# Hybrid decoder layer: three pieces of the closing RMS norm move from VectorE to GpSimd and ScalarE, and VectorE's last operations change order

## The chip, the cores and the metric

The kernel is written in Bass for one Trainium2 chip and runs on one core. The metric is the device time of one execution in microseconds, the median over runs.

## The reference

One decoder layer over 512 tokens of 1024 features in float32: block-sparse attention and a spatial-gating mixer side by side, an output projection, a squared-ReLU MLP, and last a gated per-layer embedding. Only the last three lines bear on the change:

```python
gate = jax.nn.sigmoid(jnp.einsum('bsd,de->bse', h, w_ple_gate[i]) + b_ple_gate[i])
ple = jnp.einsum('bsp,pd->bsd', p[i], w_ple[i]) * gate
h = h + rms_norm(ple, ple_post_g[i])
```

`rms_norm(x, g)` is `x * rsqrt(mean(x*x) + 1e-6) * g`, the mean over a token's 1024 features.

## The kernel before, in words

Each engine has one hand-written queue of instructions and runs it in order; semaphores tie the queues together (`wait_ge` in front of an instruction, `then_inc` behind it). Products of full float32 accuracy are made of three passes on TensorE over high and low parts. ScalarE makes the high parts, VectorE the low ones. The MLP and the gate product use a seven-product scheme over halves of tokens and features, so VectorE and ScalarE also make sums of blocks all through.

The end of the kernel is what the change touches. The gate's result, 4 groups of 128 tokens (t = 0 to 3) by 1024 columns, is finished in nine tiles, the table `GATE_TILES` (number: token group, first column): 0: t0, 0; 1: t1, 0; 2: t2, 512; 3: t2, 0; 4: t3, 512; 5: t0, 512; 6: t3, 0; 7: t1, 512; 8: t1, 768. Tiles 7 and 8 have 256 columns, the rest 512. Tile numbers follow the order in which TensorE completes them. Per tile there are six steps:

1. `sigmoid(i)` on ScalarE (L2242), out of PSUM.
2. `gate_ple(i)` on VectorE (L1463), the "gate product": sigmoid times the embedding product (`ple_late_a` for t0 and t1, `ple_late_b` for t2 and t3). Its result lies in `acc` (SBUF) for tiles 0 and 1 and in PSUM for the others.
3. `square_ple(i)` on ScalarE (L1620): sum of squares, an ACTIVATE with an accumulator read behind it.
4. On GpSimd (POOL) `partial_sum` (L2512), and once per token group `ple_rstd(t)` (L2518, L2520): 1/rms of the group's tokens, in the order t = 2, 0, 3, 1. It needs the last square of the group: 3, 5, 6, 8.
5. The "weight product": times the norm weights `ple_gain`. `gain_ple(i)` on VectorE (L1474) for tiles 2 to 8, `gain_by_pool(i)` on POOL (L2531) for tiles 0 and 1, written over `ple_late_a`.
6. `add_ple(i)` on VectorE (L1486), the "last step": h = weight product * 1/rms + h, in one scalar_tensor_tensor.

Ahead of this end VectorE runs low parts (L1409, L1432, L1376), `gate_c22` (L1440, a subtraction that completes tiles 2 and 4, the second once TensorE's product (4, 1) is done) and `gate_fold` (L1448, L1452, L1454). SyncE (SP) stores one tile per DMA (L2689), each behind its last step, in the order of `add_ple`, all on one queue. The order of all these is a list of calls per engine:

Of the kernel before, what the change touches and what calls it, by code (L numbers as in the profile page):

```python
# [35 lines left out]
ALU = mybir.AluOpType  # L36
ACT = mybir.ActivationFunctionType
# [34 lines left out]
LAST = STEPS - 1  # L72
# [16 lines left out]
GATE_COPIES = ((COPY_C11, 0), (COPY_C11, 1), (COPY_E, 0), (COPY_CHAIN, 0), (COPY_CHAIN, 1), (COPY_E, 1))  # L89
# [22 lines left out]
def gate_copy_at(which, j):  # L112

    return 3 * LAST + GATE_COPIES.index((which, j)) + 1


def gate_c22_at(j):
# [173 lines left out]
TOKENS_DONE = (2, 0, 3, 1)  # L291
# [1 line left out]


LAST_GATED = len(GATE_TILES) - 1
GAINED_BY_POOL = (0, 1)


def width_of(i):
# [16 lines left out]
def hymba_layer(nc, x, xT, pT, weights, columns, rope, ws, rows, out):  # L316
# [6 lines left out]
    with ExitStack() as ctx:  # L323
# [31 lines left out]
        h = place("h", [P, TT, D])  # L355
# [65 lines left out]
        acc = place("acc", [P, TT, D], at=at_area)  # L421
# [40 lines left out]
        def ple_of(t):  # L462
            return ple_late[t // 2][:, t % 2, :]
# [28 lines left out]
        def sem(name):  # L492
            return ctx.enter_context(nc.semaphore(name))
# [60 lines left out]
        first_load = 16  # L554
        h2_raw, gate_seeded, gate_folded = sem("h2_raw"), sem("gate_seeded"), sem("gate_folded")
        h_spilled = sem("h_spilled")
        gained_by_pool = sem("gained_by_pool")
# [165 lines left out]
        def gate_result(i):  # L723

            t, c0, width = GATE_TILES[i]
            if i == LAST_GATED:
                return psum[:, GATE_LAST_PART, 0:width]
            if t < 2:
                bank = GATE_E if c0 else GATE_P1
            else:  # L730
                bank = GATE_C22 if c0 else GATE_CHAIN
            return psum[:, bank + t % 2, 0:width]

        def gated_of(i):

            t, c0, width = GATE_TILES[i]
            return acc[:, t, 0:W] if i < 2 else gate_result(i)

        def gained_of(i):

            t, c0, width = GATE_TILES[i]
            return ple_of(t)[:, c0:c0 + width] if i in GAINED_BY_POOL else gate_result(i)

        def down_result(t):

# [9 lines left out]
        def _(dve):  # L755
# [701 lines left out]
            def gate_ple(i):  # L1457
                t, c0, width = GATE_TILES[i]
                cut = slice(c0, c0 + width)
                dve.wait_ge(sig_done, i + 1)  # L1460
                if i in (0, 2):
                    dve.wait_ge(ple_loaded[t // 2], 16)
                nc.vector.tensor_tensor(gated_of(i), gated_of(i), ple_of(t)[:, cut], ALU.mult).then_inc(pl_gated, 1)  # L1463

            GAINED = (2, 3, 4, 5, 6, 7, 8)

            def gain_ple(i):

                if i == GAINED[0]:
                    dve.wait_ge(post_loaded, 48)  # L1470
                t, c0, width = GATE_TILES[i]
                cut = slice(c0, c0 + width)
                dve.wait_ge(pl_squared, i + 1)
                nc.vector.tensor_tensor(gained_of(i), gated_of(i), ple_gain[:, cut], ALU.mult  # L1474
                                        ).then_inc(pl_gained, 1)

            def add_ple(i):

                t, c0, width = GATE_TILES[i]
                cut = slice(c0, c0 + width)  # L1480
                dve.wait_ge(pl_rstd, TOKENS_DONE.index(t) + 1)
                if i in GAINED_BY_POOL:
                    dve.wait_ge(gained_by_pool, GAINED_BY_POOL.index(i) + 1)
# [60 lines left out]
            h2_sum_split_lo(OF_S4, 1)  # L1544
            gate_ple(2)
            gate_fold(1)
            gain_ple(2)
            gate_c22(1)
            gate_ple(3)
            gate_ple(4)  # L1550
            gain_ple(3)
            gain_ple(4)
            gate_ple(5)
            add_ple(2)
            add_ple(3)
            gain_ple(5)
            gate_ple(6)
            add_ple(0)
            gate_ple(7)
            add_ple(5)  # L1560
            gain_ple(6)
            gate_ple(8)
            gain_ple(7)
            add_ple(4)
            gain_ple(8)
            add_ple(6)
            add_ple(1)
            add_ple(7)
            add_ple(8)


# [3 lines left out]
        def _(act):  # L1575
# [659 lines left out]
            def sigmoid(i):  # L2235
                t, c0, width = GATE_TILES[i]
                j = t % 2
                if t >= 2 and c0:
                    act.wait_ge(c_summed, gate_c22_at(j))
                else:  # L2240
                    act.wait_ge(up_filled, gate_at(6 if c0 else 1 if t < 2 else 5, j) + (i == LAST_GATED))
                nc.scalar.activation(gated_of(i), gate_result(i), ACT.Sigmoid).then_inc(sig_done, 1)  # L2242
# [59 lines left out]
            gate_copy(COPY_E, 1)  # L2302
            square_ple(0)
            square_ple(1)
            square_ple(2)
            sigmoid(3)
            sigmoid(4)
            square_ple(3)
            square_ple(4)
            sigmoid(5)  # L2310
            square_ple(5)
            sigmoid(6)
            sigmoid(7)
            square_ple(6)
            sigmoid(8)
            square_ple(7)
            square_ple(8)

# [4 lines left out]
        def _(pool):  # L2323
# [200 lines left out]
            def gain_by_pool(i):  # L2524
                t, c0, width = GATE_TILES[i]
                cut = slice(c0, c0 + width)
                if i == 0:
                    pool.wait_ge(post_loaded, 48)
                    pool.wait_ge(sum_lo_done, gate_sum_split_at(OF_S4, 1))
                pool.wait_ge(pl_gated, i + 1)  # L2530
                nc.gpsimd.tensor_tensor(gained_of(i), gated_of(i), ple_gain[:, cut], ALU.mult  # L2531
                                        ).then_inc(gained_by_pool, 1)

            partial_sum(0)
            partial_sum(1)
            gain_by_pool(0)
            gain_by_pool(1)
            partial_sum(2)
            ple_rstd(2)
            partial_sum(4)  # L2540
            ple_rstd(0)
            ple_rstd(3)
            partial_sum(7)
            ple_rstd(1)

# [4 lines left out]
        def _(sp):  # L2550
# [134 lines left out]
            order = (2, 3, 0, 5, 4, 6, 1, 7, 8)  # L2685
            for n, i in enumerate(order):
                t, c0, width = GATE_TILES[i]
                sp.wait_ge(out_ready, n + 1)
# [596 lines left out]
```

## Time and profile before

| | |
|---|---|
| median of 3 runs | 579.03 us (578.3 to 579.38) |
| profiled execution, its own time | 578.58 us |
| its span | 576.7 us |
| TensorE busy | 568.4 us, 99% |
| VectorE busy | 500.8 us, 87% |
| ScalarE busy | 374.9 us, 65% |
| GpSimd busy | 96.2 us, 17% |
| mean granted TensorE clock | 0.996 of full speed |

A start time and a duration on a timeline are microseconds; consecutive instructions of one engine overlap a little, so the step from start to start is shorter than the duration. The span runs from the first to the last recorded event; the execution's own time is about 1.8 us longer. "x2" merges two neighbours with one name and gives their time from first start to last end. SPq and POOLq are the queues' own records of issuing a DMA.

### The profile page before, as it was taken

The page shows a single profiled execution, that of the slowest core. Times are in us where ns is not written, and L with a number is a line of the kernel's source. Part 1 is how long each engine was busy: PE and PEld are TensorE (multiplying, and loading weights), DVE is VectorE, ACT ScalarE, POOL GpSimd, SP SyncE. Part 2 cuts the span into 40 slices and gives each one's busy share as a digit, 9 for nine tenths or more (in the row PEclk, how much of TensorE's full clock was granted, in tenths as well). Part 3 has the DMA queues.
Part 4 walks back from the last instruction along what each step waited for, and adds up shares of the span by engine and source line. Part 5 has one row for each costly group of instructions (what it writes and reads, how often), then busy time and mean ns, then how long its engine had stood idle before and what let it go on. Part 6 is the DMA issues. An engine that isn't in the chain of part 4 may idle for free.

```text
span 576.7 us, 8934 instructions
## 1 busy us (share of the span) xinstructions
PE 568.4 (99%) x3364; PEld 496.3 (86%) x3364; DVE 500.8 (87%) x645; ACT 374.9 (65%) x595; POOL 96.2 (17%) x159
## 2 busy tenths in 40 slices
PE   9999999999999999999999999999999999999995
PEld 7888888888888888899999989999998999988884
DVE  5899986688865998999999989999999899798898
ACT  6896674876555747667565565665665656686784
POOL 0321437000102501001000010011010100014122
PEclk9999999999999999999999999999999999999998
DMA  8982008223103497367476384592774853897823
GB/s 268 346 324 90 0 2 321 82 73 108 41 1 110 147 349 233 74 195 207 74 249 154 73 266 100 147 255 44 236 167 77 268 124 78 324 265 144 227 112 148
DMA packets 28603, 93.73 MB, mean 163 GB/s; under 512 B 3216, under 2 KB 4624, under 8 KB 28304
## 3 DMA queue, kind: packets, MB, share of 16 engines
q1 hardware_dynamic: 20736, 67.64, 33.0%
q0 software_dynamic: 5328, 19.14, 18.8%
q10 hardware_dynamic: 2496, 6.37, 3.1%
q8 instruction: 27, 0.44, 0.3%
q14 instruction: 16, 0.13, 0.1%
HBM read 86.85 MB, written 6.29 MB: 161 GB/s over the span
## 4 chain that ended last, share of the span: by engine, by line
PE 93%; DVE 3%; ACT 1%; issue 1%; DMA 1%; DVEq 0%; SPq 0%; ACTq 0%
PE psum L2703 29%; PE psum L2707 29%; PE psum L2708 29%; PE psum L2758 2%; PE psum L2941 2%; PE psum L2921 2%; DVE h L1486 1%; DMA first_raw_a<-weights_dram 1%; PE psum L2772 1%; DVE w_lo L1376 1%; DVE psum L1474 1%; DVE psum L1463 0%; ACT junk_late L1620 0%; PE psum L2795 0%; DVE actT_lo L1432 0%
## 5 line engine op out<-in xcount | busy, mean ns | idle before, releaser
L2703 PE MATMUL psum<-t_hi,a_hi 128*128 128x512 f32 x216 | 84.7, 392 | 0.0
L2707 PE MATMUL psum<-t_lo,a_hi 128*128 128x512 f32 x216 | 84.6, 392 | 0.0
L2708 PE MATMUL psum<-t_hi,a_lo 128*128 128x512 f32 x216 | 84.0, 389 | 0.0
L2703 PE MATMUL psum<-w_hi,actT_hi 128*128 128x512 f32 (+1 forms) x178 | 69.7, 392 | 0.0
L2708 PE MATMUL psum<-w_hi,actT_lo 128*128 128x512 f32 (+1 forms) x178 | 68.5, 385 | 0.0
L2707 PE MATMUL psum<-w_lo,actT_hi 128*128 128x512 f32 (+1 forms) x178 | 68.4, 384 | 0.0
L2708 PE MATMUL psum<-sum_hi,up_lo 128*128 128x256 f32 x224 | 63.4, 283 | 0.0
L2707 PE MATMUL psum<-sum_lo,up_hi 128*128 128x256 f32 x224 | 63.4, 283 | 0.0
L2703 PE MATMUL psum<-sum_hi,up_hi 128*128 128x256 f32 x224 | 63.2, 282 | 0.0
L2708 PE MATMUL psum<-actT_hi,up_lo 128*128 128x256 f32 (+1 forms) x200 | 60.0, 300 | 0.0
L2707 PE MATMUL psum<-actT_lo,up_hi 128*128 128x256 f32 (+1 forms) x200 | 60.0, 300 | 0.0
L2703 PE MATMUL psum<-actT_hi,up_hi 128*128 128x256 f32 (+1 forms) x200 | 59.9, 299 | 0.0
L2454 POOL DMA_DIRECT2D raw_x<-weights_dram x21 | 18.6, 883 | 238.6 <-DVE t_lo L1235 238.6
L1294 DVE TENSOR_TENSOR acc<-acc,psum 128x512 f32<-128x512 f32 x76 | 49.1, 681 | 1.8 <-PE psum L2708 1.8
L2708 PEld LDWEIGHTS psum<-t_hi,a_lo 128*128 128x128 f32 x216 | 40.6, 188 | 8.8
L1090 DVE TENSOR_TENSOR up_lo<-raw,up_hi 128x1024 fp32r<-128x1024 f32 x37 | 45.2, 1220 | 2.6 <-ACT up_hi L1881 2.0
L2703 PEld LDWEIGHTS psum<-t_hi,a_hi 128*128 128x128 f32 x216 | 40.8, 189 | 7.1
L2707 PEld LDWEIGHTS psum<-t_lo,a_hi 128*128 128x128 f32 x216 | 40.8, 189 | 6.6
L2707 PEld LDWEIGHTS psum<-sum_lo,up_hi 128*128 128x128 f32 x224 | 42.9, 191 | 1.1
L2703 PEld LDWEIGHTS psum<-sum_hi,up_hi 128*128 128x128 f32 x224 | 42.9, 191 | 1.1
L2708 PEld LDWEIGHTS psum<-sum_hi,up_lo 128*128 128x128 f32 x224 | 42.9, 191 | 0.0
L2707 PEld LDWEIGHTS psum<-actT_lo,up_hi 128*128 128x128 f32 x200 | 38.2, 191 | 2.0
(290 smaller groups left out, 1438.0 us busy)
## 6 DMA issues: line engine op xcount, KB each, us to landing
raw<-weights_dram SPq DMA_DIRECT2D x40, 512.0 KB, 4.8
raw_o<-weights_dram SPq DMA_DIRECT2D x23, 512.0 KB, 4.3
raw_x<-weights_dram POOLq DMA_DIRECT2D x21, 512.0 KB, 5.6
raw_second<-weights_dram SPq DMA_DIRECT2D x16, 512.0 KB, 4.1
raw_x<-weights_dram SPq DMA_DIRECT2D x9, 512.0 KB, 6.1
qk_raw<-weights_dram SPq DMA_DIRECT2D x8, 512.0 KB, 7.8
raw_o<-weights_dram POOLq DMA_DIRECT2D x7, 512.0 KB, 6.9
raw_second<-weights_dram POOLq DMA_DIRECT2D x6, 512.0 KB, 6.6
```

The lines of the kernel that those rows point to most:

```text
L1090: nc.vector.tensor_tensor(up_lo[q % UP_SLOTS][:], block_source(step, j), up_hi[q % UP_SLOTS][:].bitcast(F32), ALU.subtract).then_inc(block ...
L1294: nc.vector.tensor_tensor(part, part, bank, how).then_inc(product_added, 1)
L1376: nc.vector.tensor_tensor(gate_half(low, part), gate_source(block, part), gate_half(high, part).bitcast(F32), ALU.subtract).then_inc(block ...
L1474: nc.vector.tensor_tensor(gained_of(i), gated_of(i), ple_gain[:, cut], ALU.mult).then_inc(pl_gained, 1)
L1486: nc.vector.scalar_tensor_tensor(out=h[:, t, cut], in0=gained_of(i), scalar=rstd_pl[:, t:t + 1], in1=h[:, t, cut], op0=ALU.mult, op1=ALU.a ...
L2454: nc.gpsimd.dma_start(raw_x[step % 2][:], weights[down_in_stream(step, rows, half)], accum_op=ALU.add).then_inc(x_added, 16)
L2703: begin = nc.tensor.matmul(out, a_hi, b_hi, start=first, stop=False, skip_group_check=read_between)
L2707: nc.tensor.matmul(out, a_hi, b_lo, start=False, stop=False, skip_group_check=read_between)
L2708: return nc.tensor.matmul(out, a_lo, b_hi, start=False, stop=last, skip_group_check=read_between)
L2758: mm = nc.tensor.transpose(psum[:, banks[name], j * P:(j + 1) * P], source[:, j * P:(j + 1) * P], ident[:])
L2921: mm = nc.tensor.transpose(psum[:, bank + s, k * P:(k + 1) * P], probs[:, place_in_group(unit), s, k * P:(k + 1) * P], ident[:])
L2941: mm = nc.tensor.matmul(psum[s * DH:(s + 1) * DH, BANK_O, pair * P:(pair + 1) * P], v[:, k, head * DH:(head + 1) * DH], probsT_of[place_in ...
```

## The change

- Tile 2 gets its weight product on POOL (`GAINED_BY_POOL`), into `ple_late_b`; so its gate product goes to `acc` in SBUF and no longer to PSUM. ScalarE's sigmoid still writes PSUM.
- The last step of tiles 0 and 7 (`ADDED_BY_POOL`) is split in two: `scale_gained` on ScalarE multiplies by 1/rms into `ple_late_a`, `add_by_pool` on POOL adds that to h.
- VectorE's, ScalarE's and POOL's orders are rewritten around it, and SyncE stores in the order 2, 3, 5, 0, 4, 6, 1, 8, 7.

```diff
-GAINED_BY_POOL = (0, 1)
+GAINED_BY_POOL = (0, 1, 2)
+ADDED_BY_POOL = (0, 7)
+GAINED = (3, 4, 5, 6, 7, 8)
...
         def gated_of(i):
             t, c0, width = GATE_TILES[i]
+            if i == 2:
+                return acc[:, t, c0:c0 + width]
             return acc[:, t, 0:W] if i < 2 else gate_result(i)
...
             gate_ple(2)
             gate_fold(1)
-            gain_ple(2)
+            gate_ple(3)
             gate_c22(1)
-            gate_ple(3)
+            gain_ple(3)
             gate_ple(4)
-            gain_ple(3)
-            gain_ple(4)
-            gate_ple(5)
             add_ple(2)
             add_ple(3)
+            gate_ple(5)
+            gain_ple(4)
             gain_ple(5)
             gate_ple(6)
-            add_ple(0)
+            add_ple(5)
             gate_ple(7)
-            add_ple(5)
             gain_ple(6)
+            gain_ple(7)
             gate_ple(8)
-            gain_ple(7)
             add_ple(4)
             gain_ple(8)
             add_ple(6)
             add_ple(1)
-            add_ple(7)
             add_ple(8)
...
+            def scale_gained(i):
+                t = GATE_TILES[i][0]
+                act.wait_ge(pl_rstd, TOKENS_DONE.index(t) + 1)
+                if i in GAINED_BY_POOL:
+                    act.wait_ge(tail_by_pool, GAINED_BY_POOL.index(i) + 1)
+                else:
+                    act.wait_ge(pl_gained, GAINED.index(i) + 1)
+                nc.scalar.activation(scaled_of(i), gained_of(i), ACT.Copy, scale=rstd_pl[:, t:t + 1]
+                                     ).then_inc(c_copied, 1)
...
             square_ple(1)
+            sigmoid(3)
             square_ple(2)
-            sigmoid(3)
+            square_ple(3)
             sigmoid(4)
-            square_ple(3)
             square_ple(4)
             sigmoid(5)
             square_ple(5)
             sigmoid(6)
+            scale_gained(0)
             sigmoid(7)
             square_ple(6)
+            square_ple(7)
             sigmoid(8)
-            square_ple(7)
             square_ple(8)
+            scale_gained(7)
...
+            def add_by_pool(i):
+                t, c0, width = GATE_TILES[i]
+                cut = slice(c0, c0 + width)
+                pool.wait_ge(c_copied, GATE_SCALED + ADDED_BY_POOL.index(i))
+                nc.gpsimd.tensor_tensor(h[:, t, cut], scaled_of(i), h[:, t, cut], ALU.add
+                                        ).then_inc(tail_by_pool, 1)
...
             partial_sum(2)
+            gain_by_pool(2)
             ple_rstd(2)
             partial_sum(4)
             ple_rstd(0)
+            add_by_pool(0)
             ple_rstd(3)
             partial_sum(7)
             ple_rstd(1)
+            add_by_pool(7)
```

VectorE from the second fold on, in the kernel before. Tile 4's operands are in `psum` and `ple_late_b` like tile 3's, so the merged "x2" rows are gate products 3 and 4 and then weight products 3 and 4:

```order
L1454 TENSOR_TENSOR psum<-psum,acc 128x256
L1474 TENSOR_TENSOR psum<-psum,ple_gain 128x512
L1440 TENSOR_TENSOR psum<-acc,psum 128x512
L1463 TENSOR_TENSOR psum<-psum,ple_late_b 128x512 x2
L1474 TENSOR_TENSOR psum<-psum,ple_gain 128x512 x2
L1463 TENSOR_TENSOR psum<-psum,ple_late_a 128x512
L1486 SCALAR_TENSOR_TENSOR h<-psum,stat,h 128x512 x2
L1474 TENSOR_TENSOR psum<-psum,ple_gain 128x512
```

The same place with the change (L1472 is L1454 before, L1481 is L1463, L1458 is L1440, L1490 is L1474, L1502 is L1486):

```order
L1472 TENSOR_TENSOR psum<-psum,acc 128x256
L1481 TENSOR_TENSOR psum<-psum,ple_late_b 128x512
L1458 TENSOR_TENSOR psum<-acc,psum 128x512
L1490 TENSOR_TENSOR psum<-psum,ple_gain 128x512
L1481 TENSOR_TENSOR psum<-psum,ple_late_b 128x512
L1502 SCALAR_TENSOR_TENSOR h<-ple_late_b,stat,h 128x512
L1502 SCALAR_TENSOR_TENSOR h<-psum,stat,h 128x512
L1481 TENSOR_TENSOR psum<-psum,ple_late_a 128x512
L1490 TENSOR_TENSOR psum<-psum,ple_gain 128x512 x2
```

The last steps of tiles 2 and 3 (L1502) now stand ahead of gate product 5 and weight product 4.

POOL's end with the change, from partial sum 2 (L2537 is the partial sum, L2556 the weight product, L2543 and L2545 the 1/rms, L2563 the addition):

```order
L2537 TENSOR_SCALAR stat<-stat 128x1
L2556 TENSOR_TENSOR ple_late_b<-acc,ple_gain 128x512
L2543 TENSOR_SCALAR stat<-stat 128x1
L2545 TENSOR_TENSOR stat<-stat 128x1
L2537 TENSOR_SCALAR stat<-stat 128x1
L2543 TENSOR_SCALAR stat<-stat 128x1
L2545 TENSOR_TENSOR stat<-stat 128x1
L2563 TENSOR_TENSOR h<-ple_late_a,h 128x512
L2543 TENSOR_SCALAR stat<-stat 128x1
L2545 TENSOR_TENSOR stat<-stat 128x1
```

Before, the same rows stood there without L2556 and L2563. The product stands ahead of the first 1/rms, the addition between the second and the third.

ScalarE around the scaled copy of tile 0 (L2264), with the change (L2255 is the sigmoid, L1633 the square):

```order
L1633 ACTIVATE junk_late,stat<-psum 128x512
L2255 ACTIVATE psum<-psum 128x512
L2264 ACTIVATE ple_late_a<-ple_late_a,stat 128x512
L2255 ACTIVATE psum<-psum 128x256
L1633 ACTIVATE junk_late,stat<-psum 128x512
L1633 ACTIVATE junk_late,stat<-psum 128x256
L2255 ACTIVATE psum<-psum 128x256
```

These are square 5, sigmoid 6, the copy, sigmoid 7, squares 6 and 7, sigmoid 8. Before, sigmoid 7 followed sigmoid 6 directly and sigmoid 8 stood between squares 6 and 7.

## Rows read from the trace of the kernel before

**Rows 1.** The page: span, and section 1, busy time by engine.
```profile
span 576.7 us, 8934 instructions
...
PE 568.4 (99%) x3364; PEld 496.3 (86%) x3364; DVE 500.8 (87%) x645; ACT 374.9 (65%) x595; POOL 96.2 (17%) x159
```

**Rows 2.** Timeline of VectorE, 558.7 to 574.2: start, us, line, operation, [idle before, releaser].
```profile
558.73 0.68 DVE L1432 TENSOR_TENSOR actT_lo<-h2T_a,actT_hi 128x512 fp32r<-128x512 f32 x1
...
560.26 0.42 DVE L1454 TENSOR_TENSOR psum<-psum,acc 128x256 f32<-128x256 f32 x1
560.84 0.70 DVE L1474 TENSOR_TENSOR psum<-psum,ple_gain 128x512 f32<-128x512 f32 x1 [0.16 <-ACT junk_late L1620]
561.54 0.70 DVE L1440 TENSOR_TENSOR psum<-acc,psum 128x512 f32<-128x512 f32 x1
562.14 1.44 DVE L1463 TENSOR_TENSOR psum<-psum,ple_late_b 128x512 f32<-128x512 f32 x2
563.59 1.48 DVE L1474 TENSOR_TENSOR psum<-psum,ple_gain 128x512 f32<-128x512 f32 x2
564.98 0.69 DVE L1463 TENSOR_TENSOR psum<-psum,ple_late_a 128x512 f32<-128x512 f32 x1
565.57 1.40 DVE L1486 SCALAR_TENSOR_TENSOR h<-psum,stat,h 128x512 f32<-128x512 f32 x2
...
571.70 0.42 DVE L1474 TENSOR_TENSOR psum<-psum,ple_gain 128x256 f32<-128x256 f32 x1
572.03 0.74 DVE L1486 SCALAR_TENSOR_TENSOR h<-psum,stat,h 128x512 f32<-128x512 f32 x1
572.69 0.74 DVE L1486 SCALAR_TENSOR_TENSOR h<-ple_late_a,stat,h 128x512 f32<-128x512 f32 x1
573.35 0.87 DVE L1486 SCALAR_TENSOR_TENSOR h<-psum,stat,h 128x256 f32<-128x256 f32 x2
```

**Rows 3.** Timeline of ScalarE, 562.8 to 571.4.
```profile
562.87 0.60 ACT L1620 ACTIVATE junk_late<-psum 128x512 f32<-128x512 f32 x1
563.36 0.19 ACT L1620 ACTIVATION_READ_ACCUMULATOR junk_late<-psum 128x1 f32 x1
...
566.91 0.58 ACT L2242 ACTIVATE psum<-psum 128x512 f32<-128x512 f32 x1 [0.52 <-PE psum L2708]
568.34 0.37 ACT L2242 ACTIVATE psum<-psum 128x256 f32<-128x256 f32 x1 [0.85 <-PE psum L2708]
...
569.78 0.37 ACT L2242 ACTIVATE psum<-psum 128x256 f32<-128x256 f32 x1 [0.47 <-PE psum L2708]
```

**Rows 4.** Timeline of POOL, 558.7 to 564.7; the 1/rms pair comes four times.
```profile
558.79 0.68 POOL L2512 TENSOR_SCALAR stat<-stat 128x1 f32<-128x1 f32 x1 [0.63 <-ACT junk_late L1620]
559.64 2.55 POOL L2531 TENSOR_TENSOR ple_late_a<-acc,ple_gain 128x512 f32<-128x512 f32 x2 [0.17 <-POOL stat L2512]
562.16 0.21 POOL L2512 TENSOR_SCALAR stat<-stat 128x1 f32<-128x1 f32 x1
563.73 0.27 POOL L2518 TENSOR_SCALAR stat<-stat 128x1 f32<-128x1 f32 x1 [1.35 <-ACT junk_late L1620]
564.08 0.57 POOL L2520 TENSOR_TENSOR stat<-stat 128x1 f32<-128x1 f32 x1
```

**Rows 5.** Timeline of SyncE's queue, the last two stores; and its issues, size, us to landing.
```profile
573.86 0.44 SPq L2689 DMA_DIRECT2D out_dram<-h  x1
...
574.34 0.46 SPq L2689 DMA_DIRECT2D out_dram<-h  x1
...
out_dram<-h SPq DMA_DIRECT2D x2, 128.0 KB, 2.1
```

**Rows 6.** Groups by form, ScalarE and POOL, whole span: count | busy us, mean ns.
```profile
L1718 ACT ACTIVATE work<-psum,stat 128x512 f32<-128x512 f32 x2 | 1.4, 681 | 3.0 <-PE psum L2708 3.0
...
L2437 POOL TENSOR_TENSOR actT_lo<-xr,actT_hi 128x512 fp32r<-128x512 f32 x4 | 5.5, 1403 | 0.1
```

More of the change, by code:

```diff
@@ L114, in gate_copy_at @@
     return 3 * LAST + GATE_COPIES.index((which, j)) + 1
+GATE_SCALED = 3 * LAST + len(GATE_COPIES) + 1
 def gate_c22_at(j):
@@ L556, in hymba_layer @@
         h_spilled = sem("h_spilled")
-        gained_by_pool = sem("gained_by_pool")
+        tail_by_pool = sem("tail_by_pool")
         h_loaded = [sem(f"h_loaded{t}") for t in range(TT)]
@@ L736, in gated_of, with sigmoid_of @@
             t, c0, width = GATE_TILES[i]
+            if i == 2:
+                return acc[:, t, c0:c0 + width]
             return acc[:, t, 0:W] if i < 2 else gate_result(i)
+        def sigmoid_of(i):
+            return gated_of(i) if i < 2 else gate_result(i)
         def gained_of(i):
@@ L742, in gained_of, with scaled_of @@
             return ple_of(t)[:, c0:c0 + width] if i in GAINED_BY_POOL else gate_result(i)
+        def scaled_of(i):
+            t, c0, width = GATE_TILES[i]
+            return ple_of(t)[:, c0:c0 + width]
         def down_result(t):
@@ L1462, in gate_ple @@
                     dve.wait_ge(ple_loaded[t // 2], 16)
-                nc.vector.tensor_tensor(gated_of(i), gated_of(i), ple_of(t)[:, cut], ALU.mult).then_inc(pl_gated, 1)
-            GAINED = (2, 3, 4, 5, 6, 7, 8)
+                nc.vector.tensor_tensor(gated_of(i), sigmoid_of(i), ple_of(t)[:, cut], ALU.mult).then_inc(pl_gated, 1)
             def gain_ple(i):
@@ L1482, in add_ple @@
                 if i in GAINED_BY_POOL:
-                    dve.wait_ge(gained_by_pool, GAINED_BY_POOL.index(i) + 1)
+                    dve.wait_ge(tail_by_pool, GAINED_BY_POOL.index(i) + 1)
                 else:
@@ L2241, in sigmoid @@
                     act.wait_ge(up_filled, gate_at(6 if c0 else 1 if t < 2 else 5, j) + (i == LAST_GATED))
-                nc.scalar.activation(gated_of(i), gate_result(i), ACT.Sigmoid).then_inc(sig_done, 1)
+                nc.scalar.activation(sigmoid_of(i), gate_result(i), ACT.Sigmoid).then_inc(sig_done, 1)
+            def scale_gained(i):
[7 more added lines that the diff above has]
+                                     ).then_inc(c_copied, 1)
             def square_ple(i):
@@ L2531, in gain_by_pool @@
                 nc.gpsimd.tensor_tensor(gained_of(i), gated_of(i), ple_gain[:, cut], ALU.mult
-                                        ).then_inc(gained_by_pool, 1)
+                                        ).then_inc(tail_by_pool, 1)
+            def add_by_pool(i):
+                t, c0, width = GATE_TILES[i]
+                cut = slice(c0, c0 + width)
+                pool.wait_ge(c_copied, GATE_SCALED + ADDED_BY_POOL.index(i))
+                nc.gpsimd.tensor_tensor(h[:, t, cut], scaled_of(i), h[:, t, cut], ALU.add
+                                        ).then_inc(tail_by_pool, 1)
             partial_sum(0)
@@ L2684, in _ @@
             sp.dma_start(ple_late[1][:], ple_spill[:, 2:4, :]).then_inc(ple_loaded[1], 16)
-            order = (2, 3, 0, 5, 4, 6, 1, 7, 8)
-            for n, i in enumerate(order):
+            order = (2, 3, 5, 0, 4, 6, 1, 8, 7)
+            added_by_dve = [i for i in order if i not in ADDED_BY_POOL]
+            for i in order:
                 t, c0, width = GATE_TILES[i]
-                sp.wait_ge(out_ready, n + 1)
+                if i in ADDED_BY_POOL:
+                    sp.wait_ge(tail_by_pool, len(GAINED_BY_POOL) + ADDED_BY_POOL.index(i) + 1)
+                else:
+                    sp.wait_ge(out_ready, added_by_dve.index(i) + 1)
                 sp.dma_start(out[t * P:(t + 1) * P, c0:c0 + width], h[:, t, c0:c0 + width]
```

## The prediction

> **What bounds the kernel now.** I read the page first: TensorE is busy 99% of the span of 576.7 us [rows 1], so nothing upstream of its last matmul can give time back here. The edit touches only work behind the gate product, so I then read the timelines of the last 17 us, engine by engine. ScalarE shows when TensorE lets go of the last tiles: the sigmoids of tiles 6, 7 and 8 start at 566.91, 568.34 and 569.78, each released by TensorE [rows 3]. From tile 8's sigmoid to the end of the span are 7.0 us, and VectorE fills them: it works to 574.22 without a gap of note [rows 2]. Then SyncE issues the last store at 574.34, which takes 0.46 us to issue and lands 2.1 us after its issue [rows 5]. From the issue of the last store to the end of the span I count 576.74 - 574.34 = 2.40 us, with the span's 576.7 taken to the hundredth, and carry that over. So the question is when the last store is issued, and VectorE decides that now.
>
> **The change, part by part.** Steps between starts of consecutive VectorE operations (not durations) price a removed one: 0.60 us for a 512-column product (564.98 to 565.57, 561.54 to 562.14), 0.66 for a 512-column scale-and-add (572.03 to 572.69), 0.33 for a 256-column product (571.70 to 572.03), 0.39 for a 256-column scale-and-add (two take 0.87, the last one 0.48 of it) [rows 2].
> *Taken from VectorE:* the product of tile 2 with the norm weights (0.70 as it stands, 560.84 to 561.54), the last step of tile 0 (0.66), that of tile 7 (0.39): 1.75 us of 13.5.
> *Given to POOL:* one product of 1.26 us (two took 2.55 [rows 4]); an addition of 512 columns and one of 256. No addition of this shape on POOL is in the trace. I take the products' 1.26 and half of it, 0.63. Bounds for the 512 columns: from below 0.70, which VectorE takes for the same shape (560.84 [rows 2]), which would give a last issue 0.1 us earlier than below; from above 1.40, the four subtractions of L2437 [rows 6], and 2.0 with VectorE's 0.7 us of a neighbour to be waited for on top.
> *Given to ScalarE:* two scaled copies. The row with a scale from a stat column is 0.68 us for 512 columns [rows 6]; I take steps of 0.59 and 0.37 in the queue.
>
> Now in order of time.
> 1. VectorE's third gate product starts at 560.59, one 256-column step after the fold that starts at 560.26 [rows 2]; its sigmoid, moved up on ScalarE, is done by 559.3. The subtraction for tile 4 (L1440) needs TensorE's product at about 561.5 and starts as before. So taking out the 0.70 us product gives nothing yet: 0.22 us is again a wait for TensorE. Weight product 3 goes at 562.10, gate product 4 at 562.85, which waits for its sigmoid as before (before it was the second of the two at 562.14, 1.44 us for both instead of 1.29).
> 2. **The new wait.** Next on VectorE stands the last step of tile 2. It needs the 1/rms of its tokens from POOL. POOL does partial sum 2 at 562.16 and now the product of tile 2 from 562.46 to 563.75; the 1/rms chain started at 563.73 before, so its start hardly moves, and it ends at 564.65 (564.08 + 0.57) [rows 4]. VectorE reaches the step at 563.44 and waits until 564.69: 1.25 us idle. Before, weight product 4 and gate product 5 filled that stretch. At 564.69 VectorE is 0.31 us behind the old order: before, at 564.98, it had weight product 4 behind it (0.60), which now is still to do.
> 3. From there: last steps 2 and 3 (to 566.01), gate product 5 at 566.01, weight product 4 at 566.61. Weight product 5 needs square 5, which can start only when gate product 5 is done (566.73) and takes 0.68 with its accumulator read (562.87 to 563.55 [rows 3]); it goes at 567.45, 0.24 us of wait. Gate product 6 at 568.05, last step 5 at 568.65.
> 4. ScalarE now has sigmoid 6 behind square 5 (567.31 instead of 566.91). The 1/rms of tile 0's tokens is ready at 568.49 (0.92 us on POOL, plus 0.16 to be released, as at 563.73 and 564.08 [rows 3, 4]). The scaled copy of tile 0 stands in ScalarE's queue in front of sigmoid 7 and waits for it: 568.55. Sigmoid 7, ready at 568.34, starts at 569.14, 0.80 us late. Gate product 7 is late with it (569.54, 0.23 of wait), then weight products 6 and 7 (570.14, 570.74), sigmoid 8 (570.56 instead of 569.78) and gate product 8 (571.07).
> 5. POOL adds tile 0 from 569.33 to 570.63, in front of the 1/rms of tiles 4 and 6, which now ends at 571.51. VectorE wants it at 571.40 and gets it at 571.56. Then last step 4, weight product 8, last steps 6, 1 and 8 at 571.56, 572.22, 572.55, 573.21 and 573.87. VectorE ends at 574.35, where before it ended at 574.22: of the 1.75 us taken away, all is lost again in waits (0.31 carried from step 2, then 0.24, 0.23, 0.16 and the gate product's later start).
> 6. Square 8 at 571.52, the last 1/rms at 573.06, scaled copy of tile 7 at 573.12, done at 573.58, POOL's addition free to start at 573.68 and done at about 574.3. SyncE: store 1 at 574.00, store 8 at 574.40, each right behind its last step, store 7 behind store 8's issue of 0.46: 574.86 [rows 5].
>
> The same working put on the order before gives a last issue at 574.33, where the row says 574.34. So **the last store is issued 0.5 us later**, and the span becomes 574.86 + 2.40 = 577.26. The profiled execution took 578.58, 0.45 below the median 579.03 of the three runs; from it the same kernel's own time would be 579.1, and on the median it is 579.5 us.
>
> One row decides how POOL and VectorE get on. POOL's second partial sum took 0.68 us instead of the 0.21 of the third, and it ran exactly under a VectorE subtraction with two SBUF inputs (558.73 + 0.68 = 559.41; POOL 558.79 to 559.47) [rows 2, 4].
> The Trainium skill, "SBUF — State Buffer", section "SBUF: two separate sides", says that a VectorE operation with two SBUF inputs and a GpSimd operation take a shared pair of ports exclusively, so that the later one stands still for the whole of the other. By that rule, the trace agrees (0.68 against 0.21).
> Here the mechanism can bite once where it matters: last step 1 (573.21 to 573.95) reads SBUF twice, so POOL's last addition would start at 573.98 instead of 573.68 and end at 574.65 instead of 574.3. Store 7 cannot be issued before 574.86, so the sum stays, but its slack shrinks from 0.5 to 0.2 us.
>
> **The rivals.** A measurement of this kernel tells 0.2% (1.16 us) from no change; the three runs lie within 1.1 us.
> *A: as worked out,* 577.3 span, 579.5 us. For it: every wait named is on a row. Chance 0.6.
> *B: the waits are shorter and the cover holds,* so that the end is set by tile 8 alone. Sigmoid 8 at 569.78, gate product 8 at 570.18, square 8 done at 571.1, 1/rms at 572.2, last step 1 at 572.24, step 8 at 572.90, done 573.38; stores 1, 8 and 7 issued at 573.03, 573.43 and 573.89: span 576.3, 578.6 us. Against it: POOL's chain in step 2 stands on a row and the queue order in step 4 is fixed. It is the floor, and 0.45 us is no measurable gain. Chance, with all between it and A, 0.24.
> *C: slower.* POOL's addition of tile 0 stands in front of the 1/rms that VectorE waits for in step 5. From an addition of 1.1 us on, each further 0.1 us delays VectorE, and by half as much again the last addition, which then is behind store 8's slot. At 2.0 us I get a last issue at 575.81, a span of 578.2, 1.5 us more than before: 580.5 us. For it: the L2437 rows are 0.1 us longer than the products, and POOL can be held up as above. Against it: no VectorE operation under 569.33 to 570.63 has two SBUF inputs. It is measurably slower from an addition of 1.85 us. Chance 0.12.
> *D: the change does not do what it says,* because VectorE's end is not what sets the time: the last three stores, 512 KB, would leave at the rate of the transfers whatever the engines do. Then 576.7 again, 579.0 us. Against it: each of the last issues stands right behind its last step. Chance 0.04.
>
> **How the numbers follow.** The prediction is A's 579.5. Range: down to B's 578.6, up to C's 580.5. Faster by over 0.2% would need 0.7 us below the floor B, which leaves only a stray measurement: 0.03. Slower by over 0.2% is C and the far end of A: 0.14. Within 0.2%: 0.83.
>
> **What would show it.** VectorE idle for about 1.2 us ahead of its first last step (L1502), released by POOL's 1/rms; ScalarE idle ahead of the scaled copy, with sigmoid 7 at about 569.1; a VectorE wait for POOL ahead of last step 4; POOL additions of about 1.3 and 0.65 us; three stores issued back to back, the last near 574.9. I am wrong if VectorE goes through that first wait at 563.5 (toward B), if a POOL addition takes 1.8 us or more (C), or if the last issue is late with the engines early (D).

## The result, and the profile after

Over 20 runs each the changed kernel takes 579.68 us and the kernel before 578.59 us: ratio 1.0019, 95% interval 1.0013 to 1.0025, or 0.75 to 1.45 us more. The forecast was 579.5 us and +0.5 us. The time lies in the range, and the difference is within 0.2% as forecast, but it is twice the forecast one. That the forecast time of 579.5 us lies only 0.18 us from the measured one is partly luck: it started from a median of 579.03 us for the kernel before, which 20 runs put at 578.59, 0.44 lower, and it made the difference 0.57 us too small. The two errors nearly cancel.

The page of the changed kernel, against [rows 1]:

```profile
span 578.6 us, 8936 instructions
...
PE 568.4 (98%) x3364; PEld 496.4 (86%) x3364; DVE 499.1 (86%) x642; ACT 375.5 (65%) x597; POOL 101.2 (17%) x162
```

VectorE has 1.7 us less to do, as worked out, POOL 5.0 us more, of which 3.35 are its three new operations, and the span is 1.9 us longer. This profiled execution took 580.32 us, 0.64 above its median, so not all of the 1.9 is the change. To read two traces against each other I take the start of the second fold part on VectorE as zero: 560.26 in [rows 2], 560.92 here. VectorE after the change, with [idle before, releaser], against [rows 2]:

```profile
560.92 0.42 DVE L1472 TENSOR_TENSOR psum<-psum,acc 128x256 f32<-128x256 f32 x1
561.25 0.68 DVE L1481 TENSOR_TENSOR psum<-psum,ple_late_b 128x512 f32<-128x512 f32 x1
561.85 0.68 DVE L1458 TENSOR_TENSOR psum<-acc,psum 128x512 f32<-128x512 f32 x1
562.76 0.70 DVE L1490 TENSOR_TENSOR psum<-psum,ple_gain 128x512 f32<-128x512 f32 x1 [0.23 <-ACT junk_late L1633]
563.37 0.69 DVE L1481 TENSOR_TENSOR psum<-psum,ple_late_b 128x512 f32<-128x512 f32 x1
565.36 0.75 DVE L1502 SCALAR_TENSOR_TENSOR h<-ple_late_b,stat,h 128x512 f32<-128x512 f32 x1 [1.29 <-POOL stat L2545]
...
568.12 0.70 DVE L1490 TENSOR_TENSOR psum<-psum,ple_gain 128x512 f32<-128x512 f32 x1 [0.16 <-ACT junk_late L1633]
...
570.25 0.43 DVE L1481 TENSOR_TENSOR psum<-psum,ple_late_a 128x256 f32<-128x256 f32 x1 [0.17 <-ACT psum L2255]
...
573.92 0.74 DVE L1502 SCALAR_TENSOR_TENSOR h<-ple_late_a,stat,h 128x512 f32<-128x512 f32 x1
574.58 0.48 DVE L1502 SCALAR_TENSOR_TENSOR h<-psum,stat,h 128x256 f32<-128x256 f32 x1
```

VectorE stands 1.29 us in front of its first last step, for POOL's 1/rms. Then it waits for square 5 and for sigmoid 7. Ahead of all this, weight product 3 waits 0.23 us for square 3, while the subtraction (L1458) follows gate product 3 without a gap. ScalarE, where the scaled copy (L2264) waits 0.64 us and sigmoid 7 stands behind it, against [rows 3]:

```profile
567.99 0.59 ACT L2255 ACTIVATE psum<-psum 128x512 f32<-128x512 f32 x1
569.22 0.72 ACT L2264 ACTIVATE ple_late_a<-ple_late_a,stat 128x512 f32<-128x512 f32 x1 [0.64 <-POOL stat L2545]
569.85 0.36 ACT L2255 ACTIVATE psum<-psum 128x256 f32<-128x256 f32 x1
```

POOL, against [rows 4]:

```profile
563.12 1.29 POOL L2556 TENSOR_TENSOR ple_late_b<-acc,ple_gain 128x512 f32<-128x512 f32 x1
564.40 0.27 POOL L2543 TENSOR_SCALAR stat<-stat 128x1 f32<-128x1 f32 x1
564.75 0.57 POOL L2545 TENSOR_TENSOR stat<-stat 128x1 f32<-128x1 f32 x1
565.41 0.78 POOL L2537 TENSOR_SCALAR stat<-stat 128x1 f32<-128x1 f32 x1
...
570.09 1.26 POOL L2563 TENSOR_TENSOR h<-ple_late_a,h 128x512 f32<-128x512 f32 x1 [0.90 <-ACT ple_late_a L2264]
...
574.45 0.80 POOL L2563 TENSOR_TENSOR h<-ple_late_a,h 128x256 f32<-128x256 f32 x1 [0.65 <-ACT ple_late_a L2264]
```

An addition of 512 columns takes 1.26 us, as the products do. The last store, against [rows 5]:

```profile
575.57 0.46 SPq L2728 DMA_DIRECT2D out_dram<-h  x1
```

From the fold part to the last issue are 575.57 - 560.92 = 14.65 us, and 574.34 - 560.26 = 14.08 before: 0.57 later, forecast 0.52. VectorE itself ends only 0.18 us later (574.58 + 0.48 = 575.06, so 14.14, against 574.22 and 13.96). The rest is SyncE's queue: the store of tile 8 is issued right behind VectorE's end and keeps the queue until that of tile 7 can go. But from the last issue to the end of the span are now 578.59 - 575.57 = 3.02 us, where they were 2.40. That 0.6 us is what the forecast missed. The store itself lands as fast as before: SyncE's branch below stands 2.0 us behind the last issue in both. The view that shows it is that of the program's closing instructions, all on one line, L323 before and L330 now. Each row is a queue's instruction: its duration in ns, three times over, and its start in us. Before:

```profile
L323 POOLq DRAIN  x1: 3087/3087/3087, 572.6 to 572.6; - x1
...
L323 SPq COMPARE_BRANCH  x1: 38/38/38, 576.4 to 576.4; - x1
```

and after the change:

```profile
L330 POOLq DRAIN  x1: 3939/3939/3939, 574.4 to 574.4; - x1
...
L330 SPq COMPARE_BRANCH  x1: 38/38/38, 577.6 to 577.6; - x1
```

SyncE branches when its last store has landed, and each engine ends in a DRAIN. POOL's is over 3.3 us after POOL's last 1/rms before (572.58 + 3.09 = 575.67; that operation ended at 572.40), and 3.1 us after its last addition now (574.42 + 3.94 = 578.36; the addition ended at 575.25; the DRAIN's record begins while the addition still runs). Before, POOL's drain was over 0.7 us ahead of SyncE and cost nothing. Now SyncE is through at 577.6 and the program waits for POOL until 578.4.

### The profile page after: what moved, and what is told of

Its sections match the earlier page's. It is cut to its first block, busy times and chain, and to the rows that moved or that the text cites. A ratio compares the mean times of both kernels' runs of the same rounds, so it can differ in the third digit from the quotient of the medians.

```text
span 578.6 us, 8936 instructions
## 1 busy us (share of the span) xinstructions
PE 568.4 (98%) x3364; PEld 496.4 (86%) x3364; DVE 499.1 (86%) x642; ACT 375.5 (65%) x597; POOL 101.2 (17%) x162
## 4 chain that ended last, share of the span: by engine, by line
PE 86%; DMA 3%; DVE 3%; ACT 3%; POOL 2%; issue 2%; POOLq 0%; ACTq 0%; DVEq 0%
PE psum L2742 27%; PE psum L2746 26%; PE psum L2747 26%; DMA raw_second<-weights_dram 2%; PE psum L2980 2%; PE psum L2797 2%; PE psum L2960 2%; DMA raw<-weights_dram 1%; DVE w_lo L1394 1%; PE psum L2851 1%; ACT w_hi L2159 1%; PE psum L2811 1%; POOL ple_late_a L2556 0%; ACT junk_late L1633 0%; POOL stat L2379 0%
## 5 line engine op out<-in xcount | busy, mean ns | idle before, releaser
L2010 ACT ACTIVATE f<-f 128x512 f32<-128x512 f32 x21 | 13.3, 633 | 41.6 <-DVE f L1248 30.9
```

The lines of the kernel that those rows point to most:

```text
L2010: nc.scalar.activation(target, source, ACT.Relu).then_inc(relu_done, 1)
```

## The experiments

Each ran beside the kernel before on the same chip, 9 to 11 runs of each kernel and 15 to 33 of the kernel before. Differences are of medians; the interval of each ratio is about 0.5 us to either side. They ran in four groups, each on one chip with its own runs of the kernel before: the first four; the next four (idle POOL instruction, tile 7 back, both together, third product alone); then three; then the second run with the idle copy. Times are compared with the kernel before of the same group. The edits below are excerpts; "..." marks lines left out.

### The changed kernel and the kernel before, once more

No edit.

> The changed kernel once more, beside the others on one chip. Theory T (the end is longer by 0.5 us through the waits of VectorE, and the rest of the 1.1 us lies in execution-to-execution differences ahead of the end and behind the last store): +0.5 to +0.8 us on the kernel before, VectorE idle 1.2 to 1.3 us ahead of its first last step, the last store issued 15.1 us after the start of the second fold part on VectorE minus 0.5, that is 14.65 us after it (14.08 in the kernel before). Rival U (the added code slows the program elsewhere too): +1.0 us or more here, and a stage ahead of the end is longer in every profile of it.

> The kernel before under a name of its own, to see what two equal kernels differ by and how far two profiles of one kernel differ. Both theories: within 0.3 us of the kernel before; second fold part to last store issued 14.1 us. It also gives a second value for the start of the second fold part (560.26 in the first profile, 560.92 in the changed kernel's): theory T expects profiles of one kernel to differ by some tenths of a us there.

Measured: 579.69 and 578.34 us beside 578.45 for the kernel before: ratios 1.0023 (1.0014 to 1.0032) and 0.9997 (0.9988 to 1.0006). The first, +1.24 us, is above the +0.5 to +0.8 I gave, and theory T is wrong in putting the rest down to chance. In its profile the fold part starts at 560.90 and the last store is issued 14.64 us later, against 14.14 in the second profile of the kernel before, and the issue is again 3.02 us ahead of the end, against 2.41. Both halves, 0.5 and 0.6, are the same to 0.1 us in the second pair of profiles: 1.1 together, against 1.09 and 1.24 us by the medians. Neither is chance. Rival U gets its number of +1.0 us or more, but the two halves leave only about 0.1 us for it. Its sign, something longer ahead of the end, is there too: in both profiles of the changed kernel the fold part starts 0.7 to 0.9 us later than in those of the kernel before. The last section of the experiments takes that up.

### Last steps 2 and 3 back to their place

```diff
             gate_ple(4)
-            add_ple(2)
-            add_ple(3)
-            gate_ple(5)
             gain_ple(4)
+            gate_ple(5)
+            add_ple(2)
+            add_ple(3)
             gain_ple(5)
```

> The changed kernel with VectorE's last steps 2 and 3 moved behind weight product 4 and gate product 5, where they stood before; nothing else. Theory T: the wait of 1.3 us for POOL is gone, square 5 starts 1.1 us earlier, sigmoid 7 no longer stands behind the scaled copy; the last store is issued 0.9 us earlier than in the changed kernel: 0.4 us faster than the kernel before (-0.9 against the changed kernel). Rival R (the third product on POOL and the two split steps are what costs, through POOL's speed and the ports, and the order matters little): within 0.3 us of the changed kernel.

Measured: 578.71 us, 0.98 below the changed kernel on the same chip, where 0.9 was expected, and 0.26 above the kernel before, where -0.4 was (ratio 1.0003, 0.9994 to 1.0012). The rival, that the order matters little, is out. VectorE there:

```profile
562.99 0.69 DVE L1481 TENSOR_TENSOR psum<-psum,ple_late_b 128x512 f32<-128x512 f32 x1
564.43 0.70 DVE L1490 TENSOR_TENSOR psum<-psum,ple_gain 128x512 f32<-128x512 f32 x1 [0.75 <-ACT junk_late L1633]
565.04 0.69 DVE L1481 TENSOR_TENSOR psum<-psum,ple_late_a 128x512 f32<-128x512 f32 x1
565.63 0.74 DVE L1502 SCALAR_TENSOR_TENSOR h<-ple_late_b,stat,h 128x512 f32<-128x512 f32 x1
```

The 1.29 us in front of the last step is gone, 0.75 us of wait for square 4 has come in front of weight product 4, and the next three operations run through. The last store is issued 13.41 us after the fold part, 1.23 less than in the changed kernel, where the working gave 0.9, and 0.7 less than in the kernel before. That this did not become a gain is for the most part the drain: issue to end was again 3.02 us, 0.6 more than in the kernel before. That leaves -0.1 us where +0.26 was measured; the last section of the experiments takes up the remaining 0.3.

### The last store from ScalarE's queue

```diff
             scale_gained(7)
+            act.wait_ge(tail_by_pool, len(GAINED_BY_POOL) + 2)
+            t7, c7, width7 = GATE_TILES[7]
+            act.dma_start(out[t7 * P:(t7 + 1) * P, c7:c7 + width7], h[:, t7, c7:c7 + width7]).then_inc(stored, 16)
...
-            order = (2, 3, 5, 0, 4, 6, 1, 8, 7)
+            order = (2, 3, 5, 0, 4, 6, 1, 8)
```

> The changed kernel with the store of tile 7 issued by ScalarE, whose queue is empty by then, and no longer by SyncE behind the store of tile 8. Tells what the queue of stores costs by itself. Theory T: POOL's addition ends at about 575.25 on the changed kernel's own time line, so the store of tile 7 is issued 0.2 to 0.3 us earlier than 575.57, and that of tile 8 at 575.1 as before: 0.25 us faster than the changed kernel. If the transfers bounded the end instead (rival D of the prediction): no difference.

Measured: 579.68 us, level with the changed kernel's 579.69; 0.25 us was expected. The store was issued earlier, 14.37 us after the fold part instead of 14.64, but the end followed 3.31 us behind it instead of 3.02. Its transfer and SyncE's branch:

```profile
out_dram<-h ACTq DMA_DIRECT2D x1, 128.0 KB, 2.3
...
L330 SPq COMPARE_BRANCH  x1: 38/38/38, 577.9 to 577.9; - x1
```

From ScalarE's queue the store took 2.3 us to land, where those of this size took 2.1 from SyncE's. So SyncE had everything landed 577.86 - 561.19 = 16.67 us after the fold part, and 577.59 - 560.92 = 16.67 in the changed kernel: the earlier issue gave no earlier landing. POOL's DRAIN ended after that in both. So this run can't tell a limit by POOL from one by the transfers; the next one can. Why the store landed later in this run is not shown.

### One idle instruction at POOL's end

In the kernel before; the added instruction writes a number that nobody reads.

```diff
             ple_rstd(1)
+            pool.wait_ge(out_ready, 9)
+            nc.gpsimd.tensor_scalar(ple_mean, ss_pl[:, 0:1], ss_pl[:, 1:2], None, ALU.add).then_inc(pool_chain, 1)
```

> The kernel before with one more instruction at POOL's end: a 128x1 addition that waits for VectorE's last step and whose result nobody reads. In the profiles POOL's closing DRAIN ends 3.1 to 3.3 us after POOL's last operation in every kernel, and the program ends 0.2 us after the later of it and SyncE's last landing. Theory P (this drain is the second limit of the end): POOL's last operation ends at about 574.7 on the time line of the kernel before, the drain at 577.8, the span at 578.0: 1.2 us slower than the kernel before with the last store issued as before. Rival Q (the longer end of the changed kernel comes from its three stores standing close together): no difference, under 0.3 us.

Measured: 579.82 us against 578.50, ratio 1.0019 (1.0010 to 1.0028): 1.3 us for an instruction of 0.29 us, 1.2 expected. The stores are as before, last issue 14.14 us after the fold part. POOL's end:

```profile
571.70 0.57 POOL L2520 TENSOR_TENSOR stat<-stat 128x1 f32<-128x1 f32 x1
574.26 0.29 POOL L2546 TENSOR_SCALAR stat<-stat 128x1 f32<-128x1 f32 x1 [2.00 <-DVE h L1486]
```

and the closing instructions:

```profile
L323 POOLq DRAIN  x1: 3452/3452/3452, 574.2 to 574.2; - x1
...
L323 SPq COMPARE_BRANCH  x1: 38/38/38, 576.2 to 576.2; - x1
```

SyncE had everything landed at 576.2, the drain was over at 577.7, and the span is 577.9. The added instruction stands behind a wait for VectorE's last step, so POOL's last work ends at 574.55 instead of 572.3. So it is how late POOL does its last work, not what that work is, nor how close the stores stand.

### The last step of tile 7 back on VectorE

```diff
-ADDED_BY_POOL = (0, 7)
+ADDED_BY_POOL = (0,)
...
             add_ple(1)
+            add_ple(7)
             add_ple(8)
...
-            scale_gained(7)
...
-            add_by_pool(7)
...
-            order = (2, 3, 5, 0, 4, 6, 1, 8, 7)
+            order = (2, 3, 5, 0, 4, 6, 1, 7, 8)
```

> The changed kernel with the last step of tile 7 back on VectorE, ahead of that of tile 8; no scaled copy and no addition of tile 7. Theory P: the last store is issued as late as in the changed kernel (5.8 us after the last matmul starts, within 0.1), but POOL is done 2.1 us earlier, so 2.40 us and not 3.02 lie between the last issue and the end: 0.6 us faster than the changed kernel. Rival Q, or the split steps gain something for VectorE: no difference, or slower by VectorE's 0.39 us.

Measured: 579.31 us, 0.81 over the kernel before on that chip (ratio 1.0014, 1.0005 to 1.0023), where the changed kernel was 1.1 to 1.2 over it in the two groups in which it ran. In the profile the last store is issued 14.64 us after the fold part, exactly as with the addition on POOL, and the end comes 2.39 us later and not 3.02. POOL and SyncE at the end:

```profile
L330 POOLq DRAIN  x1: 3087/3087/3087, 574.2 to 574.2; - x1
...
L330 SPq COMPARE_BRANCH  x1: 38/38/38, 577.8 to 577.8; - x1
```

POOL's DRAIN is over at 577.3, 0.5 us ahead of SyncE's branch. So the split of tile 7 did not make the last store earlier, and cost 0.6 us of end. It takes 0.39 us of work from VectorE, but then the two last stores leave one behind the other, and each keeps SyncE's queue for 0.44 to 0.46 us. The median shows half of the 0.6; the changed kernel did not run on that chip, and the runs scatter by 1.5 us. By the times alone theory P and rival Q can't be told apart (0.3 to 1.3 us over the kernel before, against 0.8 to 1.85 and 0.75 to 1.45 for the changed kernel); the profile tells them apart.

### Both together, twice

The edits of "last steps 2 and 3 back" and "tile 7 back on VectorE" in one kernel.

> Both together: last steps 2 and 3 behind weight product 4 and gate product 5, and tile 7 back on VectorE. Theory P: 0.9 and 0.6 us off the changed kernel, so 1.5 faster than it. Against the kernel before the end has become 0.4 us shorter; what the time shows of it depends on ScalarE's wait for the second half of the weights' block of L2159 at 539 us, which was 0.2 to 0.3 us in two profiles of the kernel before and 0.6 to 1.3 in four of the changed family. If that is chance of an execution: 0.3 to 0.4 us faster than the kernel before. If it belongs to the changed family: the same as the kernel before, within 0.2 us.

> The best version once more, on this chip and beside the kernel before: 0.2 to 0.5 us faster than it (first time 578.11 against 578.50); the second fold part to the last store issued 13.4 us, against 14.1. A second look also at the wait at 539 us: 0.6 us or more again if it belongs to the family.

Measured: 578.11 against 578.50 us (ratio 0.9994, 0.9985 to 1.0003) and, on another chip, 578.15 against 578.51 (0.9997, 0.9988 to 1.0006). Each set against the kernel before on its own chip, this is 1.5 to 1.6 us less than the changed kernel, as expected. Against the kernel before it is 0.4 less by the medians of both groups, and neither interval excludes zero. From fold part to last issue the profiles show more, 13.41 and 13.42 us against 14.1, and 2.4 behind it. But the fold part itself starts later in this version, which takes half of it or more back; the last section of the experiments has the numbers. The wait at 539 us was 0.63 and 1.42 us; the time that the expectation gives for a long wait, level with the kernel before, is not what the medians show. This is the fastest version of this study. That it beats the kernel before is likely and not shown.

### The third product alone, and the split of tile 0 alone

The first has the tile 2 product on POOL and no split last step, the second the reverse. Each has more than the lines shown. The first has the changed kernel's places for gate product 3, weight product 3, sigmoids 3 and 4 and squares 2 and 3. The second has its order of VectorE, ScalarE and the stores from last step 5 on: last step 5 ahead of gate product 7, weight product 7 ahead of gate product 8, square 7 ahead of sigmoid 8.

```diff
-GAINED_BY_POOL = (0, 1)
+GAINED_BY_POOL = (0, 1, 2)
```

> The kernel before with only the product of tile 2 on POOL (and gate product 3 and sigmoid 3 as in the changed kernel), last steps all on VectorE. Theory: the time of that product turns into a wait for square 4 on VectorE, so it gives nothing: the last store is issued as in the kernel before, within 0.1 us of 4.9 us after the last matmul starts. Rival: 0.6 us faster, the time of the product. The wait at 539 us, as in the expectation of the run before, tells whether it follows from this part of the change already.

```diff
+            scale_gained(0)
...
+            add_by_pool(0)
...
-            add_ple(0)
```

> Of the change only the split last step of tile 0 (scaled copy on ScalarE, addition on POOL), with the third product on VectorE and the last steps in the places that served best. Theory: the product on POOL gave VectorE nothing but a wait, so this ends exactly like the run with both (last store 4.2 us after the last matmul starts if the wait at 539 us is short, 4.55 if it is as in the changed family), 0.4 us below the kernel before or level with it. Rival: without the third product it is 0.6 us slower than the run with both.

Measured: 578.49 us against 578.50 for the third product alone (1.0004, 0.9995 to 1.0013), last issue 14.16 us after the fold part: nothing. 578.27 against 578.51 for the split of tile 0 alone (0.9992, 0.9983 to 1.0001), last issue after 13.53, 0.6 below the kernel before and 0.12 above the version with both. The rival, 0.6 us slower without the third product, is out. VectorE in the run with the third product alone:

```profile
561.46 0.69 DVE L1458 TENSOR_TENSOR psum<-acc,psum 128x512 f32<-128x512 f32 x1 [0.33 <-PE psum L2745]
...
564.25 0.70 DVE L1490 TENSOR_TENSOR psum<-psum,ple_gain 128x512 f32<-128x512 f32 x1 [0.75 <-ACT junk_late L1635]
```

The product taken from VectorE, a step of 0.60 us, has become wait: 0.33 us for TensorE and 0.75 for square 4. The kernel before has some waits there as well (0.16 and about 0.1 us around the product), and gate product 5 starts 4.75 us after the fold part, where it started after 4.72. So what the change can give lies in the split of tile 0 together with the order from there on; no run separates these two.

### An idle instruction at ScalarE's end, twice

The profiles held one more difference. At about 539 us ScalarE waits for the second half of a block of weights that POOL's queue accumulates into `raw_second`. Before and after the change:

```profile
539.14 1.06 ACT L2146 ACTIVATE w_hi<-raw_second 128x1024 fp32r<-128x1024 f32 x1 [0.28 <-DMA raw_second<-weights_dram]
```

```profile
539.80 1.06 ACT L2159 ACTIVATE w_hi<-raw_second 128x1024 fp32r<-128x1024 f32 x1 [1.32 <-DMA raw_second<-weights_dram]
```

The wait was 0.6 to 1.5 us in all six profiles with the scaled copy of tile 0 that I had, 0.3 or less in the four without. With a long wait the fold part starts 8.65 to 8.85 us ahead of the last matmul's start, otherwise 9.2 to 9.3, so VectorE's end begins 0.4 to 0.6 us later. The change touches nothing ahead of it but the length of the programs. I put one instruction behind ScalarE's last in the kernel before:

```diff
             square_ple(8)
+            act.wait_ge(pl_squared, 9)
+            nc.scalar.activation(junk_late[:, 0:1], ss_pl[:, 0:1], ACT.Copy)
```

> The kernel before with one 128x1 copy more at ScalarE's end, behind its last square, where nothing waits for it. It can do nothing to the end: the last store is issued 4.9 us after the last matmul starts, 2.4 us before the end. It tests whether the longer wait for weights at 539 us (0.6 to 1.5 us in six profiles with the scaled copy of tile 0, 0 to 0.3 in four without) comes with the length of ScalarE's program. Theory L (it does): that wait is 0.6 us or more here and the time 0.3 to 0.4 us over the kernel before. Rival: wait under 0.35 us, time within 0.2 us of it.

> The kernel before with the idle copy at ScalarE's end, a second time, since one profile and an interval of 1.8 us in 2000 do not settle 0.3 us. Theory L (the wait for weights at 539 us grows with ScalarE's program): wait 0.6 us or more in this profile too, time 0.2 to 0.5 us over the kernel before. Rival (the first was a stray execution): wait under 0.35 us, time within 0.2 us.

Measured: first 578.88 against 578.51 us with a wait of 1.21, which looked like theory L; then, on another chip, 578.49 against 578.55 with no wait at all. The theory falls: the length of ScalarE's program doesn't set it. The further runs with the scaled copy had 1.19 and 1.42. So 8 profiles with that copy show 0.63 us or more, and 5 of 6 without it 0.28 or less, and I have no cause for it. It stays open. It would fit that four versions with the copy came out about 0.3 us above what their ends say ("last steps 2 and 3 back" +0.26 where 13.41 + 3.02 gives -0.1; tile 7 back on VectorE +0.8 where its end gives +0.5; both together -0.4 where it gives -0.7; the split of tile 0 alone -0.2 where it gives -0.5). But the changed kernel itself does not: +1.09 and +1.24 where its ends give 1.2 and 1.1.

Two things limit what this can mean. In all six profiles with a wait of 1.17 us or more the profiled execution took 0.6 to 0.9 us more than its kernel's median. With 0.63 or 0.64 us it stood at the median, twice. (The changed kernel's second profile, with 0.69, lay 0.7 above.) So a wait of over 1 us was seen only in slower executions, and a typical one may well have less. And the start of the fold part is not a quite neutral zero: in the first run with the idle copy, whose end is that of the kernel before, the last issue comes 13.94 us after it, with the long wait, and in the second after 14.15, without. Tenths between profiles of the two kinds are uncertain by 0.2 us. Counted from the start of the last matmul instead, the last issue comes 4.87 and 4.88 us later in the kernel before, 4.56 and 4.77 with both together, and 4.86 with the split of tile 0 alone.

## Why the prediction was right or wrong

**The waits in VectorE's queue: right from step 2 on.** Step 2 put 1.25 us of idle time in front of the first last step; it is 1.29. Step 3 put weight product 5 at 7.19 us after the fold part, and it is at 7.20. Step 4 put sigmoid 7 at 8.88, and it is at 8.93. Step 5 had VectorE's end 14.09 us behind the fold part's start, and it is at 14.14 (575.06). Step 6 had the last issue at 14.60, measured 14.65 and 14.64. VectorE stood 0.15 us for POOL ahead of last step 4, as step 5 had it (the step from gate product 8 is 0.48 us and not 0.33). Putting the last steps back took 0.98 us off the time and 1.23 off the last issue, 0.9 by the same working.

Step 1 came out by luck. It has VectorE wait for TensorE in front of the subtraction (L1440) and weight product 3 go 1.84 us after the fold part. It went after 1.84 us, but the subtraction did not wait, since the fold part started closer to TensorE's end. It was square 3 that held weight product 3, by 0.23 us. With the third product alone, where the fold part started early, the wait for TensorE was there, with 0.33 us.

**The shared ports: the row held twice more.** POOL's partial sum of 565.41 took 0.78 us instead of 0.22, under VectorE's last step 2, which has two SBUF inputs and ran until 566.11. With last steps 2 and 3 back, nothing on VectorE with two SBUF inputs ran beside it, and it took 0.22. Its last addition took 0.80 us: it was dispatched at 574.45, 0.21 ahead of the end of last step 1 (574.66), and ended 0.59 after it. The Trainium skill, "SBUF — State Buffer", section "SBUF: two separate sides", says that such a pair takes the shared ports exclusively, so that the later one stands still until the other is through; the trace agrees, with ends 0.08 and 0.59 us behind VectorE's.

**The step that failed is the one in the first part:** "From the issue of the last store to the end of the span I count 576.74 - 574.34 = 2.40 us ... and carry that over". The 2.40 us is a property of SyncE's chain alone. The program's end waits for POOL too, as the idle instruction at its end shows (1.3 us), and POOL's closing DRAIN needs 3.1 us behind POOL's last operation. The change moved that operation 2.2 us later, from 12.14 us behind the fold part to 14.33. In step 6 I worked out when it would end, and asked only whether it would be in time for the store. The missing term: 14.33 + 3.11 + 0.23 = 17.67 us, with 0.23 from the DRAIN's end to the span's, against 14.65 + 2.40 = 17.05 for the stores, so 0.6 us. With it the forecast would have been +1.1 us, the measured difference.

**The rivals.** B's shorter waits did not come. C's mechanism did not come either, since POOL's addition took 1.26 us and not 1.85. What came is a loss on the same engine that C didn't name: not how long POOL's work takes, but that it is the last. D is excluded: the time changed, each store again left behind its last step or the issue before it, and in the changed kernel all had landed 1.0 us before the end. The idle POOL instruction adds 1.3 us with the stores unchanged. The chance of 0.14 for slower by more than 0.2% was too low: with the missing term the working gives +1.1 us, right beside the border of 1.16 us, which the measured interval of 0.75 to 1.45 us takes in.

**What is not explained** is the wait at 539 us, which goes with a start of VectorE's end that is 0.4 to 0.6 us later in a single execution, and the 0.3 us by which four versions with the scaled copy lie above what their ends give.

## What to carry to other kernels

Before work moves to an idle engine at the end of a program, write down for each engine when it does its last operation and how long its closing instructions take: here POOL needed 3.1 us behind its last operation, so POOL had to be done 0.9 us before the last store was even issued (2.4 us from that issue to the end, less 3.1 and 0.2). In a queue that is run in order, an operation taken out gives only what stands behind it and is ready: of 1.75 us taken from VectorE, the product of 0.70 gave 0 and 0.1 us of last issue in the two comparisons made, the last step of tile 7 gave nothing because the stores then queued, and two last steps placed 1.2 us too early cost 1.0 us. Read the queue behind each removed instruction for what it waits for, before counting its time as a gain.

## What the runs showed of the hardware that was not expected

POOL's closing DRAIN ended 3.11 us after POOL's last operation in the five profiles in which that operation was an addition behind a wait with nothing after it (changed kernel twice, its two versions with tile 7 on POOL, the idle instruction), and 3.27 us after it in the nine where it was the 1/rms pair with a wait behind it. VectorE's and ScalarE's DRAINs ended within 0.1 us of their last operation, except ScalarE's in the run in which it issued the last store. The program ended 0.21 to 0.23 us after the later of POOL's and SyncE's DRAIN, in all 14 profiles. An instruction of 0.29 us at POOL's end, behind a wait for VectorE's last step, lengthened the program by 1.3 us.
